# 24 matmuls of 256 columns in place of 16 wide ones, and GELU read straight from PSUM, in the expert up tiles of a two-layer kernel

## The reference

```python
def retrieve(args):
    xc, ic, gc = args
    uc = u_tab[ic]
    vc = v_tab[ic]
    hdn = jax.nn.gelu(jnp.einsum('cd,chkd->chk', xc, uc).astype(jnp.float32), approximate=False) * gc
    return jnp.einsum('chk,chkd->cd', hdn.astype(vc.dtype), vc)
```

## Time and profile before

| what | value |
|---|---|
| median of 3 runs | 2127.34 us (2124.79 to 2127.45) |
| the profiled execution's own time | 2127.19 us |
| its span, first to last instruction | 2125.4 us |
| around the span | 1.8 us |
| mean granted clock | 0.916 |
| expert part (797 to 1513 us) | 716 us, a third of the span |

### The profile page before, as it was taken

The page is one execution under the profiler, slowest core; times in us unless marked ns, Lnnn a source line. Parts: engine busy times, 40 slices in busy tenths (PEclk is TensorE's granted clock), DMA queues, the critical chain, the costliest instruction groups (busy, mean ns, idle before and its releaser), DMA issues.

```text
span 2125.4 us, 31363 instructions
## 1 busy us (share of the span) xinstructions
PE 1738.9 (82%) x10422; PEld 1529.9 (72%) x10422; DVE 1453.7 (68%) x2596; ACT 789.4 (37%) x1369; POOL 340.3 (16%) x245
## 2 busy tenths in 40 slices
PE   2978468687602669999999999999799995878998
PEld 2977357576602668888888888888699853668998
DVE  5898755434698767888888888766535845437886
ACT  1433410102300235555555555555345212504443
POOL 1974400000003980000000000000004301500000
PEclk8999779988855889999999999999899997999999
DMA  7964000033300005777777777655354351023553
GB/s 293 327 227 165 12 0 1 1 109 119 109 0 0 0 10 185 238 237 238 233 237 235 236 238 236 215 189 187 118 170 157 119 190 39 1 79 132 185 179 118
DMA packets 91213, 306.14 MB, mean 144 GB/s; under 512 B 10128, under 2 KB 10512, under 8 KB 90768
## 3 DMA queue, kind: packets, MB, share of 16 engines
q1 hardware_dynamic: 90576, 301.99, 43.0%
q10 hardware_dynamic: 576, 3.36, 0.4%
HBM read 304.26 MB, written 1.05 MB: 144 GB/s over the span
## 4 chain that ended last, share of the span: by engine, by line
PE 67%; DVE 22%; POOL 5%; issue 3%; DMA 2%; ACT 1%; SPq 0%; POOLq 0%; ACTq 0%; DVEq 0%
PE bank L463 10%; PE bank L1460 5%; PE bank L1462 5%; PE bank L1464 5%; PE bank L464 5%; PE bank L448 5%; PE bank L449 5%; PE bank L450 5%; DVE arena L751 3%; POOL arena L1409 3%; PE bank L424 3%; PE bank L1421 2%; PE bank L474 2%; PE bank L1241 1%; PE bank L467 1%
## 5 line engine op out<-in xcount | busy, mean ns | idle before, releaser
L442 DVE TENSOR_TENSOR wlo<-wring,whi 128x1024 fp32r<-128x1024 f32 x360 | 438.6, 1224 | 121.4 <-ACT whi L437 111.6
L437 ACT CAST whi<-wring 128x1024 fp32r<-128x1024 f32 x414 | 432.3, 1046 | 37.4 <-PE bank L450 17.9
L448 PE MATMUL bank<-xboth,whi 128*128 128x256 f32 x1088 | 315.2, 290 | 37.7 <-DVE wlo L442 22.0
L463 PE MATMUL bank<-xboth,whi 128*128 128x512 f32 x896 | 323.2, 399 | 3.6 <-DVE wlo L442 3.6
L449 PE MATMUL bank<-xboth,whi 128*128 128x256 f32 x1088 | 311.2, 286 | 0.0
L450 PE MATMUL bank<-xboth,wlo 128*128 128x256 f32 x1088 | 311.0, 286 | 0.0
L442 POOL TENSOR_TENSOR wlo<-wring,whi 128x1024 fp32r<-128x1024 f32 x54 | 156.9, 2925 | 874.3 <-ACT whi L437 874.3
L464 PE MATMUL bank<-xboth,wlo 128*128 128x256 f32 x896 | 252.2, 281 | 0.0
L448 PEld LDWEIGHTS bank<-xboth,whi 128*128 128x128 f32 x1088 | 212.4, 195 | 43.0 <-issue 31.9
L449 PEld LDWEIGHTS bank<-xboth,whi 128*128 128x128 f32 x1088 | 212.5, 195 | 0.7 <-issue 0.7
L450 PEld LDWEIGHTS bank<-xboth,wlo 128*128 128x128 f32 x1088 | 212.3, 195 | 0.0
(11 more groups left out here) (351 smaller groups left out, 2955.1 us busy)
## 6 DMA issues: line engine op xcount, KB each, us to landing
wring<-in_w SPq DMA_DIRECT2D x463, 512.0 KB, 3.6
arena<-in_ada SPq DMA_DIRECT2D x48, 512.0 KB, 5.0
xn<-in_ada SPq DMA_DIRECT2D x96, 256.0 KB, 3.1
wring<-in_w SPq DMA_DIRECT2D x6, 384.0 KB, 3.0
wring<-in_w SPq DMA_DIRECT2D x9, 256.0 KB, 2.6
hT<-in_xT SPq DMA_DIRECT2D x1, 1024.0 KB, 9.3
arena<-in_subk ACTq DMA_DIRECT2D x1, 1024.0 KB, 4.9
out_hT<-hT SPq DMA_DIRECT2D x1, 1024.0 KB, 3.9
```

Of the source, the lines that this page charges most:

```text
L437: act.copy(whi[:, n % HSLOTS, :], wring[:, n % SLOTS, :]).then_inc(hi_ready, 1)
L442: eng.tensor_tensor(wlo[:, n % SLOTS, :], wring[:, n % SLOTS, :], whi[:, n % HSLOTS, :].bitcast(F32), ALU.subtract).then_inc(lo_ready, 1)
L448: pe.matmul(out, h, xh, start=start, stop=False, **kw)
L463: pe.matmul(out, h, xboth[:, k, :, :], start=(k == 0), stop=False)
```

## The change

`wide8` is gone. An up tile is made by `split8`, in 24 matmuls of 256 columns into the bank's first 256 columns. With it go ScalarE's copy, VectorE's sum and their two semaphores; GELU reads the bank. TensorE's wait for a free bank is on `gelu_ready`. Down tiles are as they were.

```diff
-        def wide8(pe, out, n):
-
-            for k in range(KT):
-                h, l = whi[:, n % HSLOTS, k * 128:k * 128 + 128], wlo[:, n % SLOTS, k * 128:k * 128 + 128]
-                if k < KT - 1:
-                    pe.matmul(out, h, xboth[:, k, :, :], start=(k == 0), stop=False)
-                    pe.matmul(out[:, 0:S], l, xhi[:, k, :], start=False, stop=False)
-                else:
-                    pe.matmul(out[:, 0:S], l, xhi[:, k, :], start=False, stop=False)
-                    mm = pe.matmul(out, h, xboth[:, k, :, :], start=False, stop=True)
-            return mm
...
-        h_rest, h_summed, gelu_ready, w_gated, w_hi, w_ready = (sem("h_rest"), sem("h_summed"), sem("gelu_ready"),
-                                                                sem("w_gated"), sem("w_hi"), sem("w_ready"))
+        gelu_ready, w_gated, w_hi, w_ready = sem("gelu_ready"), sem("w_gated"), sem("w_hi"), sem("w_ready")
...
             def up(j, n, split, free):
                 pe.wait_ge(lo_ready, split)
                 if free is not None:
-                    pe.wait_ge(h_summed, free)
-                wide8(pe, bank[j % 3][:, :], n).then_inc(tile_done, 1)
+                    pe.wait_ge(gelu_ready, free)
+                split8(pe, bank[j % 3][:, 0:S], n).then_inc(tile_done, 1)
...
                 act.wait_ge(tile_done, 6 * i + (n + 1))
                 if j >= 3:
                     act.wait_ge(w_ready, 3 * i + (j - 2))
-                act.copy(ge[:, j % 3, :], bank[j % 3][:, S:2 * S]).then_inc(h_rest, 1)
-                act.wait_ge(h_summed, 3 * i + (j + 1))
-                act.activation(ge[:, j % 3, :], ge[:, j % 3, :], ACT.Gelu).then_inc(gelu_ready, 1)
+                act.activation(ge[:, j % 3, :], bank[j % 3][:, 0:S], ACT.Gelu).then_inc(gelu_ready, 1)
...
                 if j > 0:
                     lo(n + 2, i)
-                dve.wait_ge(h_rest, 3 * i + (j + 1))
-                dve.tensor_tensor(ge[:, b, :], bank[j % 3][:, 0:S], ge[:, b, :], ALU.add).then_inc(h_summed, 1)
                 dve.wait_ge(gelu_ready, 3 * i + (j + 1))
```

## The result

The changed kernel takes 2130.62 us in the median of 10 runs (2129.05 to 2135.56), the kernel before 2124.53 us in 10 runs, among which are the three that the forecast started from. The ratio is 1.0034 with a 95% interval of [1.0022, 1.0045]: slower by about a third of a per cent, some 7 us (the two medians are 6.1 us apart). In a second comparison, with three other kernels on one chip, it was 1.0023 [1.0010, 1.0036]. The ratios here are of the runs in the chip's fast state, which leaves out two runs of kernels further down, one of 4729.73 us (count alone) and one of 5891.32 us (ends alone). Its profiled execution has a span of 2133.7 us, 8.3 more than before.

A forecast was written before the change was run, and what follows sets the result against it. TensorE's gapless matmuls were taken to bound the expert part. Up tiles +8.6 us, exposed chains -1.16 and -0.43, sum +7.0 on 2127.19 gives 2134.2 us; range about 3 us down and 4 up.

The forecast's parts named there:

- TensorE is the bound, and the other engines' savings buy nothing: Expert part: matmuls follow without gaps, so less ScalarE and VectorE work in a turn gains 0.
- Up tile 2.88 in place of 2.8125, 127 times, +8.6: Expert part's up tiles: 24 steps of 0.1200 us cost 0.0675 us more a tile, +8.6 us in all.
- Exposed chains, -1.16 and -0.43: TensorE's waits before down(0) and down(127) at the expert part's ends vanish, gaining 1.16 and 0.43 us.
- Sum +7.0: Whole kernel: +8.6 - 1.16 - 0.43 = +7.0 us, giving 2134.2 us, 0.33% more.
- VectorE's busy time -53 us: Sign in the profile after: in the expert part VectorE's busy time falls by about 53 us, ScalarE's by about 48.
- The reason given, a fixed 13 to 16 ns beside the columns: Up tile: each matmul adds 13 to 16 ns beside its columns at 2.4 GHz, with 8 more matmuls a tile.
- Columns alone: Rival for the up tile: time goes with its 6144 columns, turn stays 5.5525 us, 2125.6 us in all; chance 0.05.
- Quicker step: Rival for the up tile: 256-column steps take 0.115 us, 0.0525 less a tile, 2118.9 us in all; chance 0.05.
- Dearer step: Rival for the up tile: steps take 0.1225 us, +0.1275 a tile, 2141.8 us in all; chance 0.07.
- Waits that stay at the ends: Rival at the expert part's ends: waits stay, sum +8.6 to +7.7, 2135.8 to 2134.9 us; within the forecast's 0.83.

The follow-up runs named there:

- count alone: Kernel before with up tiles of 24 matmuls of 256 columns, copy and sum kept: ratio 1.0032 [1.0018, 1.0045], expert part +8.38 us.
- ends alone: Kernel before with only up tiles 0 and 127 changed to 24 matmuls and GELU from the bank: ratio 0.9989 [0.9974, 1.0003], expert part -1.48 us.
- GELU alone: Kernel before with its 16 matmuls, GELU reading the bank, copy and sum gone: ratio 0.9977 [0.9963, 0.9991], expert part -1.82 us.

## Why the prediction was right

- *TensorE is the bound, and the other engines' savings buy nothing.* Shown: turns of 5.55 with and without copy and sum.
- *Up tile 2.88 in place of 2.8125, 127 times, +8.6.* The count alone gave +8.38. The turn of 5.62 was met to the hundredth. The step read in two other stages held here, with other transfers and another neighbour. 8.38 / 127 is 0.066 us a turn, within the rounding of the rows.
- *Exposed chains, -1.16 and -0.43.* GELU alone gave -1.82 for -1.59, and both waits were gone. The table load went into the idle time behind the Silu, as taken; GELU from the bank takes 0.39 us, for the 0.42 assumed. The missing 0.2 us is for the most part the slower start of the pair behind a wait: 0.70 us in the earlier trace rows, 0.63 without one. I had counted the idle time only.
- *Sum +7.0.* Measured 6.64 in the part, and 2130.62 for 2134.2 forecast, which is 3.6 us less where the working allowed about 3. Most of it is the baseline: the three runs that the forecast started from (median 2127.34) lay high among the ten (2124.53), by 2.8 us. The ratio forecast, 1.0033, was met, and that the measured 1.0034 comes so near is partly luck, since its interval is 0.0023 wide and the second comparison gave 1.0023.
- *VectorE's busy time -53 us* was off: 44. The sum was 53.8 us of instructions, but busy time counts overlapping instructions once, and the changed stretch takes in one cast more (1.2 us). ScalarE's 46 stands for 48.
- *The reason given, a fixed 13 to 16 ns beside the columns*, is right only as a description of 256 and 512 columns at a granted clock of 1.00. The runs put in its place a floor of 0.111 us a step, a share of the weight load at 256 columns (6 ns of the 13) that isn't there at 512, and about 5 ns for a pair of different widths. The last also explains why four more matmuls (12 to 16, 2.72 to 2.81 us) cost more than eight more (16 to 24, 2.81 to 2.88): at 13 ns each the four cost 0.053 us and the eight 0.107, but the first step brings eight pairs of unlike widths, 0.04 us, and the second takes them away.
- *Rivals.* Columns alone: refuted by +8.38. Quicker step: 0.1200 and not 0.115. Dearer step: refuted, 0.1200 and not 0.1225; the wide tile's 16 ns contained the change of width. Waits that stay at the ends: refuted.

## What to carry to other kernels

Where one engine is gapless, price a change by that engine's start-to-start step for the exact shape, read where the same shape already runs back to back; removing work from engines that wait is worth only what it takes off the few places where their chain is exposed, and those can be treated alone (here 2 tiles of 128). At one number of columns, fewer and wider matmuls win, and like widths should stand together. Below 256 columns there is little left to gain by narrower matmuls: with a weight load of 128 columns, 192 columns cost what 128 do, 0.110 and 0.111 us against 0.120.

## What the runs showed of the hardware that was not expected

- At a granted clock of 1.00 a step with a full weight load stops falling at about 0.111 us: 0.110 at 192 columns, 0.111 at 128. At 0.50 steps of 128, 192 and 256 columns all take 0.213.
- Alternating 512 and 256 columns costs about 5 ns a pair more than the two among their likes (0.3516 against 0.3467 us); seven wide and eight narrow ones in a row give it back.
- A 512-column pair right behind narrow steps takes longer the narrower they are: 0.47 us behind 256 columns, 0.49 behind 192, 0.53 behind 128, and 0.45 behind its like. The first narrow step behind wide ones is the shorter, 0.09 us in place of 0.11 with 192 columns.
- From one execution to the next the same unchanged stages ahead of the part moved its first matmul between 788.2 and 798.7 us, and up tile 0, in the kernels with up to 24 matmuls a tile, took 4.34 to 5.50 us with the moment at which the granted clock rose. A stretch counted from behind that moment agreed to 0.01 us between two profiles. In four of the other kernels the rise came only after the first read.
